# Gate dot products moved under the MLP, two split steps swapped, lambda loaded as columns, x loaded first

## The reference, cut to what matters

```
c_act = silu(c)
mod = c_act @ ada_w[layer] + ada_b[layer]
shift_t, scale_t, gate_t, shift_m, scale_m, gate_m = split(mod, 6)
h = modulate(rms_norm(x, norm_g[layer, 0]), shift_t, scale_t)
x = x + gate_t * mixer(h)
h = modulate(rms_norm(x, norm_g[layer, 1]), shift_m, scale_m)
x = x + gate_m * (square(relu(h @ w1)) @ w2)
lam = exp(sum(lp[0] * lp[1])) - exp(sum(lp[2] * lp[3])) + lam_init   # lp = b_lambda, 4 x 128
```

## Time and profile before

| | us |
|---|---|
| median of 3 runs | 2374.14 (2373.33 to 2374.79) |
| the profiled execution, its own time | 2374.41 |
| its span in the profile | 2372.6 |
| PE busy | 2342.0, 99% of the span |
| DVE busy | 1768.1, 75% |
| ACT busy | 1242.7, 52% |
| mean share of full TensorE clock granted | 0.997 |

### The profile page before, as it was taken

The page is one execution under the profiler, slowest core; times in us unless marked ns, Lnnn a source line. Parts: engine busy times, 40 slices in busy tenths (PEclk is TensorE's granted clock), DMA queues, the critical chain, the costliest instruction groups (busy, mean ns, idle before and its releaser), DMA issues.

```text
span 2372.6 us, 28881 instructions
## 1 busy us (share of the span) xinstructions
PE 2342.0 (99%) x11309; PEld 1937.5 (82%) x11309; DVE 1768.1 (75%) x2291; ACT 1242.7 (52%) x2162; POOL 52.7 (2%) x74
## 2 busy tenths in 40 slices
PE   7999999999999999999999999999999999999999
PEld 4468888888888888888888888877888888888887
DVE  6678878888999878888898887858875555555554
ACT  3166566667535534534546666654653553553542
POOL 1000000001000000000001210000100000000000
PEclk9999999999999999999999999999999999999999
DMA  9987777966999888798886877657875555555554
GB/s 393 424 333 297 303 293 300 379 233 248 368 397 367 331 301 336 290 342 307 328 338 235 340 298 271 240 179 277 323 277 195 187 191 192 192 189 195 187 193 153
DMA packets 151000, 665.38 MB, mean 280 GB/s; under 512 B 17392, under 2 KB 17872, under 8 KB 121424
## 3 DMA queue, kind: packets, MB, share of 16 engines
q1 hardware_dynamic: 150864, 663.53, 75.0%
HBM read 661.33 MB, written 2.13 MB: 280 GB/s over the span
## 4 chain that ended last, share of the span: by engine, by line
PE 87%; DMA 5%; DVE 5%; ACT 3%; issue 1%; POOL 1%; SPq 0%; DVEq 0%; ACTq 0%
PE main L533 18%; PE main L428 16%; PE main L430 16%; PE main L429 16%; PE main L535 9%; DMA qT<-ada 3%; PE main L442 2%; PE main L444 2%; PE main L443 2%; DVE w_lo L1335 1%; DVE ada_raw L1342 1%; DMA subg_sb<-subg 1%; DVE qT L1342 1%; PE tr L584 1%; PE tr L533 1%
## 5 line engine op out<-in xcount | busy, mean ns | idle before, releaser
L906 ACT ACTIVATE w_hi<-w_raw 128x1024 fp32r<-128x1024 f32 x771 | 793.8, 1055 | 548.1 <-DMA w_raw<-w 545.0
L1335 DVE TENSOR_TENSOR w_lo<-w_raw,w_hi 128x1024 fp32r<-128x1024 f32 x771 | 921.6, 1220 | 213.1 <-ACT w_hi L906 211.0
L1342 DVE CUSTOM_DVE_ANT_0 ada_raw<-ada_raw,c_row,biasc 128x2048 f32<-128x2048 f32 x208 | 492.0, 2365 | 31.2 <-DMA ada_raw<-ada 30.0
L533 PE MATMUL main<-hT,w_hi 128*128 128x512 f32 x1856 | 464.7, 392 | 0.0
L533 PEld LDWEIGHTS main<-hT,w_hi 128*128 128x128 f32 x1856 | 334.3, 189 | 60.1
L428 PE MATMUL main<-w_hi,mid_hi 128*128 128x512 f32 x960 | 373.5, 389 | 0.0
L429 PE MATMUL main<-w_lo,mid_hi 128*128 128x512 f32 x960 | 373.5, 389 | 0.0
L430 PE MATMUL main<-w_hi,mid_lo 128*128 128x512 f32 x960 | 373.4, 389 | 0.0
L428 PE MATMUL main<-w_hi,hT 128*128 128x512 f32 x848 | 338.7, 399 | 1.8 <-ACTq L950 0.8
L430 PE MATMUL main<-w_hi,hT 128*128 128x512 f32 x848 | 330.8, 390 | 0.0
L429 PE MATMUL main<-w_lo,hT 128*128 128x512 f32 x848 | 330.1, 389 | 0.0
(11 more groups left out here) (270 smaller groups left out, 1884.2 us busy)
## 6 DMA issues: line engine op xcount, KB each, us to landing
w_raw<-w SPq DMA_DIRECT2D x800, 512.0 KB, 4.4
ada_raw<-ada SPq DMA_DIRECT2D x208, 1024.0 KB, 6.8
qT<-ada SPq DMA_DIRECT2D x16, 1024.0 KB, 12.3
gate<-gate_rows SPq DMA_DIRECT2D x4, 1024.0 KB, 8.3
xs<-x SPq DMA_DIRECT2D x1, 2048.0 KB, 7.6
out<-xs SPq DMA_DIRECT2D x3, 512.0 KB, 6.5
out<-xs SPq DMA_DIRECT2D x2, 256.0 KB, 2.6
st_a<-lamb SPq DMA_DIRECT2D x1, 256.0 KB, 17.9
```

The costliest lines, as they stand in the source:

```text
L533: pe.matmul(banks[f][:, :], w_hi[:, s, wc], hT[:, :, kt, :], start=(kt == 0), stop=False)
L906: act.activation(w_hi[:, s, :], w_raw[:, s, :], ACT.Copy).then_inc(hi_done, 1)
L1335: dve.tensor_tensor(w_lo[:, s, :], w_raw[:, s, :], w_hi[:, s, :].bitcast(F32), ALU.subtract).then_inc(lo_done, 1)
L1342: dve.tensor_tensor_reduce(piece, piece, c_row[:, :], gain, biasc[:, section, kt:kt + 1], ALU.mult, ALU.add, out).then_inc(ada_used, 1)
```

## The change

- `ADA_Q`: three loads and dot products of kv chunk 0 (pieces 0, 3, 6) become one (piece 7). `ADA_V`: one each is taken from chunks 10 and 11 (the pieces 6 and 5). `ADA_GATE_B`: four more in chunk 3 of the last MLP's first block. So four dot products move from the attention to the MLP; the write and read of gate 2 move from kv chunk 2 to 4, and those of gate 3 from pieces 1 and 4 of chunk 3 to piece 7 of chunk 3 and piece 1 of chunk 4.
- Lambda is loaded as `lamb4`, 128 partitions by 4 numbers (2 KB), one product of columns on VectorE, one matmul against `ones` for the sums over the partitions, one copy. The broadcast of 256 KB and the two reductions in `angles` go.
- SP issues `x` ahead of `biasc`, and `lamb4` behind it. VectorE copies its half of `c_row` ahead of waiting for the biases.
- TensorE's first `qk_transposes` come after piece 2 of the first `gemm`, not after piece 1.
- In kv chunk 8, heads 2 and 3 are rounded and split ahead of weight piece 4 on ScalarE and VectorE, and TensorE transposes heads 4 and 5 after its third piece, not its second.
- `load_sqrt` is put ahead of the first `sub_stats` of chunk 9.
- The statistics of query chunk 3 use `sc` and `ov` as scratch, so that `modulate_kept` waits for one root fewer.
- `skip` shrinks from 192 to 176 numbers for the two new small tiles.

```diff
-ADA_Q = after((), (0, 5, 7), (0, 5, 7), (0, 5, 7), (0, 3, 6), (0, 5, 7), (0,))
-ADA_V = after((6, 7), (5, 7), (0, 6), (5, 7), (0, 6), (1, 2), (), (5, 6), (4, 5, 6), (0, 2, 5), first=2)
-ADA_GATE_B = after((1, 3, 5, 7), (0, 2, 4, 6), (0, 2, 4, 6))
+ADA_Q = after((), (0, 5, 7), (0, 5, 7), (0, 5, 7), (7,), (0, 5, 7), (0,))
+ADA_V = after((6, 7), (5, 7), (0, 6), (5, 7), (0, 6), (1, 2), (), (5, 6), (4, 5), (0, 2), first=2)
+ADA_GATE_B = after((1, 3, 5, 7), (0, 2, 4, 6), (0, 2, 4, 6), (0, 1, 3, 4))
...
             sp.dma_start(cols_in[0:96, :], vecs_in).then_inc(vec_in, 16)
+            sp.dma_start(xs[:, :, :], x_in.rearrange("(t p) d -> p t d", p=P)).then_inc(x_in_done, 16)
             sp.dma_start(biasc[:, :, :], bias_cols_in).then_inc(bias_in, 16)
-            sp.dma_start(xs[:, :, :], x_in.rearrange("(t p) d -> p t d", p=P)).then_inc(x_in_done, 16)
+            sp.dma_start(lamb4[:, :], lamb_in).then_inc(lamb_in_done, 16)
...
-            sp.dma_start(st_a[:, 0:NC], lamb_in.partition_broadcast(P)).then_inc(small_in, 16)
...
-            gate_steps = {2: {3: lambda: gate_write(2), 6: lambda: gate_read(2, 4 + 16)}}
+            gate_steps = {4: {3: lambda: gate_write(2), 6: lambda: gate_read(2, 4 + 16)}}
...
-            gate_steps = {3: {1: lambda: gate_write(3), 4: lambda: gate_read(3, 4 + 16 + 4)}}
+            gate_steps = {3: {7: lambda: gate_write(3)}, 4: {1: lambda: gate_read(3, 4 + 16 + 4)}}
...
             spread_c()
+            pe.wait_ge(lamb_paired, 1)
+            claim_tr(0)
+            pe.matmul(tr[0][:, 0:2], ones[:, :], lamb2[:, :], start=True, stop=True).then_inc(lamb_summed, 1)
             pe.wait_ge(turn_ready, 1)
...
-                gemm(0, *h, side={1: [qk_transposes], 5: [qk_transposes]})
+                gemm(0, *h, side={2: [qk_transposes], 5: [qk_transposes]})
...
-                                  1: [head_transposes(4, heads), head_transposes(5, heads)],
+                                  2: [head_transposes(4, heads), head_transposes(5, heads)],
...
-                chunk(PIECES, {4: [qk_stats(1 - ch % 2)], 5: [qk_scale(1 - ch % 2)],
+                chunk(PIECES, {4: [qk_stats(1 - ch % 2, places=(sc, ov) if ch == 3 else None)], 5: [qk_scale(1 - ch % 2)],
...
-            chunk(PIECES, {3: heads[0:2], 4: [values(1), exps_of(0), exps_of(1)], 5: heads[2:4], 6: heads[4:6], 8: [move_pt]})
-            chunk(PIECES, {1: [sub_stats], 2: [sub_stats], 4: [heads[6]], 5: [heads[7]]})
+            chunk(PIECES, {3: heads[0:2], 4: [values(1), exps_of(0), exps_of(1), *heads[2:4]], 6: heads[4:6], 8: [move_pt]})
+            chunk(PIECES, {1: [load_sqrt, sub_stats], 2: [sub_stats], 4: [heads[6]], 5: [heads[7]]})
...
+            dve.wait_ge(lamb_in_done, 16)
+            dve.tensor_tensor(lamb2[:, :], lamb4[:, 0::2], lamb4[:, 1::2], ALU.mult).then_inc(lamb_paired, 1)
+            dve.wait_ge(lamb_summed, 1)
+            dve.tensor_copy(lam[:, 0:2], tr[0][:, 0:2]).then_inc(tr_free[0], 1)
+            dve.wait_ge(tr_free[0], 3)
+            dve.sem_inc(lam_dot, 1)
             dve.wait_ge(c_spread, 4)
...
-            section_chunk(8, {2: [causal[0], negate_max(0)], 3: lows[0:2], 4: [causal[1], negate_max(1)], 5: [*lows[2:4], mix(0)], 6: [*lows[4:6], mix(1)],
+            section_chunk(8, {2: [causal[0], negate_max(0)], 3: lows[0:2],
+                              4: [causal[1], negate_max(1), *lows[2:4]], 5: [mix(0)], 6: [*lows[4:6], mix(1)],
...
-            modulate_kept((S_SCALE_KV, S_SHIFT_KV), 4 * PIECES, 4 * GROUPS + 3)
+            modulate_kept((S_SCALE_KV, S_SHIFT_KV), 4 * PIECES, 4 * GROUPS + 2)
```

More of the change, by code:

```diff
@@ L212, in trunk @@
         turns = sb("turns", [P, T * HALF])
+        lamb4 = sb("lamb4", [P, 4])
+        lamb2 = sb("lamb2", [P, 2])
         scratch = sb("scratch", [P, 1])
@@ L217, in trunk @@
         pos_i = sb("pos_i", [P, T], I32)
-        sb("skip", [P, 192])
+        sb("skip", [P, 176])
         with nc.sbuf_tensor("mid_hi", [P, KT, T * P], F32R) as mid_hi, \
@@ L263, in trunk @@
         ada_used = sem("ada_used")
+        lamb_in_done, lamb_paired, lamb_summed = sem("lamb_in_done"), sem("lamb_paired"), sem("lamb_summed")
         c_ready, c_wide, c_spread = sem("c_ready"), sem("c_wide"), sem("c_spread")
@@ L1674, in _ @@
             dve.tensor_scalar(residue[:, :], residue_i[:, :], 0.0, NEG, ALU.is_gt, ALU.mult).then_inc(residue_done, 1)
+            for q in range(2, 4):
+                dve.wait_ge(c_wide, q + 1)
+                dve.tensor_copy(c_row[:, cols(q, NC)], c_banks[q][:, :]).then_inc(c_spread, 1)
             dve.wait_ge(bias_in, 16)
@@ L1679, in _ @@
             chained(last)
-            for q in range(2, 4):
-                dve.wait_ge(c_wide, q + 1)
-                dve.tensor_copy(c_row[:, cols(q, NC)], c_banks[q][:, :]).then_inc(c_spread, 1)
+            dve.wait_ge(lamb_in_done, 16)
[4 more added lines that the diff above has]
+            dve.sem_inc(lam_dot, 1)
             dve.wait_ge(c_spread, 4)
@@ L1687, in angles @@
             def angles():
[L1689 to L1693, removed]
+                dve.wait_ge(small_in, 16)
                 chained(dve.tensor_copy(pos_f[:, :], pos_i[:, :]))
@@ L2040 @@
         "subg": f["b_subln_g"].reshape(-1),
-        "lamb": f["b_lambda"].reshape(-1),
+        "lamb": f["b_lambda"].reshape(4, HD).T,
         "ada": np.concatenate([w.reshape(-1, D) for w in (first, *by_column[2:])]),
```

## The result

The changed kernel takes 2360.29 us (median of 4 runs, 2360.07 to 2360.54), the kernel before 2374.38 beside it: ratio 0.9941, interval 0.9929 to 0.9953.

The account below looks back on a forecast made before the run. TensorE was taken to bound the kernel, busy 2342.0 of 2372.6 us, so only its waits could be won. Terms -1.5-1.3-1.2-1.3-1.2-4.4 = -10.9 from 2374.4 gave 2363.5 us, range 2361.0 to 2368, chance 0.72.

Parts of the forecast that it names:

- 1. The start: Start of the kernel: the small lambda load replacing the broadcast shortens the DMA stream; -1.5 us, between -2.0 and 0.
- 2. First query transposes: First query chunk: transposes one piece later remove TensorE's wait for the rotated queries; -1.3 us, between -1.8 and -0.5.
- 3. kv chunk 0: kv chunk 0: fewer dot products stop holding `kept_low`; -1.2 us, between -1.5 and 0; GpSimd's root edit worth 0.
- 4. and 5. Heads and root table: Heads 2 and 3 ahead of a weight, -1.3 us; early root table, -1.2 us; each removes a TensorE wait.
- 6. Chunks 10 and 11: Chunks 10 and 11: both TensorE waits for `w_lo` and the clock's fall go; -4.4 us, between -4.5 and -2.
- ScalarE's wait below 6: Sign to look for: ScalarE's 10.29 us wait for a weight, ending at 1623.95, should shrink below 6.
- clock 1.00 between 1600 and 1660: Sign to look for: TensorE's clock at 1.00 from 1600 to 1660 us, where it had fallen to 0.66 in 1640 to 1645.
- 7. The last MLP: Last MLP, chunk 3: four added dot products of 2.35 us each fit without making TensorE wait; cost 0.
- (c): Rival, chance 0.04: the four dots only move the wait to the gate's read in the MLP; 2368.5 us.
- (a): Rival, chance 0.12: the start gives nothing, from slow small rows or VectorE's later start; -9.4, 2365.0 us.
- (b): Rival, chance 0.10: TensorE still waits in chunk 11, losing 3 us, and kv chunk 0 loses 1.2; 2367.7 us.
- (d): Rival, chance 0.02: slower, TensorE's clock stays at half through the unrounded pieces, 28 to 130 us; 2412 us.

Follow-up runs that it names:

- e11: The changed kernel with the whole old start back (lambda broadcast of 256 KB, two reductions, biases ahead of x, old preamble order): 2363.10 us, +2.8.
- e12: The kernel before with the new start alone: 2372.17 us against 2373.73 for the kernel before beside it, ratio 0.9993.
- e13: The changed kernel with an added 256 KB broadcast read from lambda's own 2 KB tensor: 2362.25 us, +2.2 against the changed kernel on the same chip.
- e6: The changed kernel with the dot products of (10, 6) and (11, 5) back, two fewer in the last MLP: 2366.19 us, +5.9.
- e7: The changed kernel with heads 2 and 3 behind weight piece 4 again, and TensorE's transposes of heads 4 and 5 after its second piece: 2362.23 us, +1.9.
- e9: The changed kernel with the first query transposes one piece earlier again: 2361.63 us, +1.3.
- e5: The changed kernel with kv chunk 0's three dot products back in place of the one behind piece 7, two fewer in the last MLP: 2363.55 us, +3.3.
- e10: The changed kernel with GpSimd waiting for the fourth root again and query chunk 3's statistics on their old scratch: 2360.53 us.
- e15: The changed kernel with one more dot product in kv chunk 0, behind piece 3, one fewer in the last MLP: 2360.82 us, +0.8 against 2360.04.
- e1: The changed kernel with an added 256 KB broadcast, read from a row of x, behind the positions: 2361.53 us, +1.2.
- e2: The changed kernel with an added load of 256 KB from 128 different rows of x: 2360.69 us, +0.4.

## Why the prediction was right or wrong

Sign, mechanisms and the list of waits that go were right. Every term that counted was too small but the second, which was too large, and the bounds of four parts (the start, kv chunk 0, the heads, chunks 10 and 11) were too tight.

*1. The start: the term that was mis-sized most.* Forecast -1.5 with a bound of -2.0; -2.8 in the traces, -2.3 to -2.8 by e11. Only e12's median, -1.6 from runs that spread over 3.9, would leave the 1.5 standing; its trace has -2.8. The step that failed is the price of the broadcast: I worked it out from the shortfall of one window and took 1.5 out of a span of 0.6 to 2.0, with the positions' part inside it. The interval between the landings around it holds all of it: 2.0 us for a load of 0.6 us of bytes (e13, e11). The remaining 0.3 to 0.8 are not assigned to an edit. The price put on VectorE's preamble was too high: `turn` was forecast 0.85 later, and came 0.2 later. The changed kernel, VectorE's timeline, against the earlier trace rows:

```profile
10.90 0.51 DVE L1686 SCALAR_TENSOR_TENSOR biasc<-biasc,vec 128x16 f32<-128x16 f32 x5
11.44 0.16 DVE L1690 TENSOR_TENSOR lamb<-lamb 128x2 f32<-128x2 f32 x1
12.08 0.16 DVE L1692 COPY lam<-tr 128x2 f32<-128x2 f32 x1 [0.48 <-PE tr L771]
12.64 2.35 DVE L1348 CUSTOM_DVE_ANT_0 ada_raw<-ada_raw,c_row,biasc 128x2048 f32<-128x2048 f32 x1 [0.40 <-DVE lam L1692]
...
17.65 0.48 DVE L1631 TENSOR_SCALAR gate<-ident,rstdx 128x128 f32<-128x128 f32 x2
```

The round trip of 0.48 was as forecast, but the rest of the preamble ran shorter and earlier, so the first dot product came 0.9 later, not 1.4. The cover, TensorE's slack behind the DMA stream, holds: in the profiles of e6 and e7 the first transposes ran 0.9 and 1.0 later than in the changed kernel, and at 105 us 0.2 and 0.0 of it were left. What the Trainium skill says in "DMA: Bandwidth & Descriptors", Specifications, on rows under 512 bytes did not shrink the gain: the new load of 16-byte rows lands 0.2 after the biases (7.2 us from its issue at 2.16, against 7.5 from 1.66), and the landings are ahead by more than forecast.

*2. First query transposes.* -1.6 and then +1.0 back by 250 us, net -0.6 (e9's trace says the same) where I took -1.3. "Some tenths at the pieces 5 and 6" was the step that was too small: 0.9 came in its place, 0.3 of it at 154 us and 0.5 at 189 us. They are there in e11 too, and without them in e9 the first wait is back.

*3. kv chunk 0.* -1.9 (e5: 2.0) against a bound of -1.5. The hidden part was under-counted: the shown waits, some tenths for a third and 0.16 for each made 1.4, and the stretch was late by 0.5 more. The step that failed is the 0.16; the rows of e5 show 0.27. GpSimd's root was worth 0 (e10). I wrote that the chain loses 2.3 for each dot product; the rows show 2.3 for the one behind piece 0 and 1.2 for the one behind piece 3, and e15 shows that TensorE feels it only past a margin.

*4. and 5. Heads and root table.* -1.6 and -1.3 by the traces, 1.6 and 1.3 when undone, against -1.3 and -1.2. Wait plus 0.16 gave 1.36 for the heads; a quarter of a microsecond was missing.

*6. Chunks 10 and 11.* -5.0 and -0.4 behind it, against -4.4. Its sum was 2.8 for waits and 1.7 for the clock. e6 shows that the second is not a cost of its own: at full clock the time goes into a third wait, and the three shown waits of 4.2, with 0.27 more for each, make 5.0. What one loses is VectorE's split chain, with or without the clock's fall. The marker "ScalarE's wait below 6" was missed (6.52), "clock 1.00 between 1600 and 1660" held.

*7. The last MLP.* 0, as forecast. The last dot product starts at 1741.89 and the gate's read is issued at 1747.29 and takes 6.3 us: it lands 5.7 ahead of 1759.3, when it is wanted (1773.7 less the 14.4 gained). So (c) did not come; nor did (a), (b) or (d): the clock is at 0.50 in 20 to 22 us as before and no later wait returned.

Errors of one sign add up: 1.3 at the start, 0.7 in kv chunk 0, 0.6 + 0.4 in chunk 11, 0.4 in heads and table, 1.0 by chance, less 0.7 in part 2, make 3.7, against the 3.5 between the forecast's sum and the traces' (the rest is rounding). The low end of 2361.0 fell although it lay 0.9 below all best ends together (2374.4 less 12.5 is 2361.9): holding the bounds to be unlikely together did not matter, the bounds themselves were too tight. By the gain of 13.3 the forecast was 2.4 short and not 3.2. In rival (b) half of part 3 is 0.6 and not 1.2, so it stood 0.6 too high.

## What to carry to other kernels

Price a small load by the interval between the landings of its neighbours, not by its bytes or by one slow window; a broadcast of a 2 KB tensor to 128 partitions took three times its bytes' time. Undo each edit by itself and read it at its place, since the median of single edits can stand a microsecond off. Price a wait from the rows on both sides of it, not from the idle time shown. When a slow clock lies behind a wait, ask whether the engine would have stood anyway: the slow stretch and the next wait may be one loss, not two.

## What was not expected of the hardware

- Two broadcasts of 256 KB at the same place, of the same form, cost 1.2 us when read from a row of a 2 MB tensor and 2.2 when read from a tensor of 2 KB (e1, e13); the same bytes from 128 rows cost 0.4 (e2). Why the source matters is not settled: no run varied the small tensor's size or address.
- The same wait of 2.2 us of TensorE was followed by a granted clock of 0.66 in 1640 to 1645 us in the kernel before and by 1.00 in e6 and e12, although the wait ahead of it is the same too (0.36 in the kernel before, 0.38 in e12). Why is open.
- A matmul of 512 columns that had waited was itself followed after 0.34 us at full clock, not after 0.23 (both waits of e5's kv chunk 0 and all three of e6).
- In 17 of the 18 profiles one load between 31 and 43 us lands 0.4 to 1.6 later than the stream's pace, not always the same load. With it the lateness after the start differs by about a microsecond from profile to profile.
